# Down projections that read and write their 384 token columns in runs of 32

## The reference

```
def half_ffn(x, shift, scale, gate, g, w_gu, w_down):
    h = modulate(x, g, shift, scale)              # RMS norm, then scale and shift
    a, u = jnp.split(h @ w_gu, 2, axis=-1)        # w_gu: 1024 x 5632
    return x + FFN_RES * gate * ((jax.nn.silu(a) * u) @ w_down)    # w_down: 2816 x 1024

for i in range(DEPTH):
    xp = half_ffn(xp, ..., ff1_w_gu[i], ff1_w_down[i]);  xs = half_ffn(xs, ...)
    xp, xs = token mixer i (windowed, global, latent-compressed or neighbourhood attention)
    xp = half_ffn(xp, ..., ff2_w_gu[i], ff2_w_down[i]);  xs = half_ffn(xs, ...)
```

## Time and profile before

| what | value |
|---|---|
| median of 3 runs | 2933.23 us |
| span of the profiled execution, first to last instruction | 2931.5 us |
| median less that span | 1.7 us |
| PE busy | 2900.1 us, 99% of the span, 17613 matmuls |
| DVE busy | 2274.4 us, 78% |
| ACT busy | 1252.3 us, 43% |
| DMA, mean of the core's 16 engines | 167 GB/s |
| matmuls of the down projections | 3 x 1408 = 4224 |

### The profile page before, as it was taken

How to read it: one execution, slowest core, us unless ns; L and a number is a source line. 1 busy time by engine, 2 the same in 40 slices (tenths; PEclk the granted TensorE clock), 3 DMA queues, 4 the chain that set the end, 5 groups by cost and what they waited for, 6 DMA issues and landing times.

```text
span 2931.5 us, 44455 instructions
## 1 busy us (share of the span) xinstructions
PE 2900.1 (99%) x17613; PEld 2810.0 (96%) x17613; DVE 2274.4 (78%) x3459; ACT 1252.3 (43%) x2001; POOL 166.6 (6%) x171
## 2 busy tenths in 40 slices
PE   8999999999999999999999999999999999999999
PEld 6999979999999998999999997899999999989999
DVE  6889887888787877888788777778888887777653
ACT  3332464443333266443333348644333333664432
POOL 0000220000000030000000012000000001320000
PEclk9999999999999999999999999999999999999999
DMA  7555314555455512455455531255555555324342
GB/s 290 208 211 216 145 42 170 187 201 204 181 190 190 217 56 93 186 193 210 180 191 199 198 120 46 73 201 193 199 190 192 193 207 195 108 75 173 128 143 93
DMA packets 87722, 490.22 MB, mean 167 GB/s; under 512 B 11824, under 2 KB 13168, under 8 KB 51376
## 3 DMA queue, kind: packets, MB, share of 16 engines
q1 hardware_dynamic: 83696, 480.42, 44.4%
q0 software_dynamic: 3904, 8.24, 1.1%
HBM read 485.33 MB, written 3.29 MB: 167 GB/s over the span
## 4 chain that ended last, share of the span: by engine, by line
PE 55%; issue 38%; DVE 4%; ACT 1%; DMA 1%; POOL 1%; SPq 0%; DVEq 0%; POOLq 0%; ACTq 0%
PE ps L840 16%; PE ps L859 8%; PE ps L845 8%; PE ps L880 5%; PE ps L1060 4%; PE ps L863 4%; PE ps L824 1%; PE ps L995 1%; PE ps L1035 1%; DMA boot<-in_mod_w 1%; PE ps L1134 1%; PE ps L976 1%; PE ps L980 1%; DVE tmp L1685 0%; PE ps L1079 0%
## 5 line engine op out<-in xcount | busy, mean ns | idle before, releaser
L840 PE MATMUL ps<-h_hi,w_hi 128*128 128x386 f32 x2688 | 908.2, 338 | 0.0
L840 PE MATMUL ps<-h_lo,w_hi 128*128 128x386 f32 x2688 | 893.4, 332 | 0.0
L1593 DVE TENSOR_TENSOR w_lo<-w_raw,w_hi 128x2048 fp32r<-128x2048 f32 (+3 forms) x282 | 706.9, 2507 | 30.0 <-ACT w_hi L1263 29.6
L1613 DVE CUSTOM_DVE_ANT_0 F_junk<-F_slab,cond,mod_b 128x1024 f32<-128x1024 f32 x544 | 707.2, 1300 | 12.7
L1263 ACT ACTIVATE w_hi<-w_raw 128x2048 fp32r<-128x2048 f32 (+4 forms) x278 | 578.7, 2082 | 14.8 <-DMA w_raw<-in_ffn_dn 10.8
L840 PEld LDWEIGHTS ps<-h_lo,w_hi 128*128 128x128 f32 x2688 | 512.5, 191 | 0.0
L840 PEld LDWEIGHTS ps<-h_hi,w_hi 128*128 128x128 f32 x2688 | 503.1, 187 | 0.4 <-ACT w_hi L1263 0.4
L845 PE MATMUL ps<-h_hi,w_lo 128*128 128x386 f32 x2688 | 494.4, 335 | 0.0
L859 PE MATMUL ps<-F_act_hi,w_hi 128*128 128x384 f32 x1408 | 473.6, 336 | 0.0
L859 PE MATMUL ps<-F_act_lo,w_hi 128*128 128x384 f32 x1408 | 473.3, 336 | 0.0
L845 PEld LDWEIGHTS ps<-h_hi,w_lo 128*128 128x128 f32 x2688 | 469.0, 187 | 0.0
(11 more groups left out here) (371 smaller groups left out, 3465.9 us busy)
## 6 DMA issues: line engine op xcount, KB each, us to landing
w_raw<-in_ffn_gu SPq DMA_DIRECT2D x176, 1024.0 KB, 4.8
F_slab<-in_mod_w SPq DMA_DIRECT2D x272, 512.0 KB, 5.6
w_raw<-in_ffn_dn SPq DMA_DIRECT2D x64, 1408.0 KB, 6.4
w_raw<-in_d_w SPq DMA_DIRECT2D x8, 1536.0 KB, 6.7
boot<-in_mod_w SPq DMA_DIRECT2D x8, 1024.0 KB, 10.2
w_raw<-in_a_w SPq DMA_DIRECT2D x4, 1536.0 KB, 6.6
w_raw<-in_b_w SPq DMA_DIRECT2D x4, 1536.0 KB, 6.7
w_raw<-in_c_w SPq DMA_DIRECT2D x8, 544.0 KB, 3.6
```

The costliest lines, as they stand in the source:

```text
L840: pe.matmul(ps[:, 2 * par + u, 0:N_MOVE], w[0][:, k, u, :], h[:, k, :], start=(k == 0 and h is h_hi), stop=False)
L1593: dve.tensor_tensor(w_lo[par][:, 0:w], w_raw[par][:, 0:w], w_hi[par][:, 0:w], ALU.subtract).then_inc(w_split_lo.sem, 1)
L1613: dve.tensor_tensor_reduce(out=junk[:], in0=w, in1=cond[:, c, :], scale=scale, scalar=mod_b[:, n:n + 1], op0=ALU.mult, op1=ALU.add, accum_ ...
```

## The change

The function `combed` is new. It takes a tile of 384 consecutive columns and gives a view of the same columns in another order: four groups, and in each group a run of 32 columns of token tile 0, then one of tile 1, then one of tile 2. In the second feed-forward of a layer (`s % 3 == 2`) the groups rise: columns 0-31, 128-159, 256-287, then 32-63, 160-191, 288-319, and so on. In the first one (`s % 3 == 0`) they fall: 96-127, 224-255, 352-383, then 64-95, and so on. Within a run the columns always rise. The view is used for both the moving operand and the PSUM output, so each column still lands where it did. Weights, waits, semaphores, buffers and DMAs are as before.

```
+RUN = 32
...
+def combed(z, s):
+    n = P // RUN
+    step, at = (-RUN, (n - 1) * RUN) if s % 3 == 0 else (RUN, 0)
+    return bass.AP(tensor=z.tensor, offset=z.offset + at, ap=[list(z.ap[0]), [step, n], [P, TT], [1, RUN]])
...
                     for y in (act_hi, act_lo):
-                        pe.matmul(ps[:, B_DN[par], 0:N_TOK], w_hi[par][:, k * P:(k + 1) * P],
-                                  y[:, k * N_TOK:(k + 1) * N_TOK], start=(k == 0 and y is act_hi), stop=False)
+                        pe.matmul(combed(ps[:, B_DN[par], 0:N_TOK], s), w_hi[par][:, k * P:(k + 1) * P],
+                                  combed(y[:, k * N_TOK:(k + 1) * N_TOK], s), start=(k == 0 and y is act_hi), stop=False)
                 pe.wait_ge(w_split_lo.sem, w_split_lo.after(s, c))
                 for k in range(KF):
-                    mm = pe.matmul(ps[:, B_DN[par], 0:N_TOK], w_lo[par][:, k * P:(k + 1) * P],
-                                   act_hi[:, k * N_TOK:(k + 1) * N_TOK], start=False, stop=(k == KF - 1))
+                    mm = pe.matmul(combed(ps[:, B_DN[par], 0:N_TOK], s), w_lo[par][:, k * P:(k + 1) * P],
+                                   combed(act_hi[:, k * N_TOK:(k + 1) * N_TOK], s), start=False, stop=(k == KF - 1))
```

## The result

| | before | after |
|---|---|---|
| median | 2933.35 us (9 runs, 2932.97 to 2933.96) | 2941.15 us (9 runs, 2940.93 to 2941.92) |
| ratio | | 1.0026, 95% interval 1.0017 to 1.0036 |
| span of the profiled execution | 2931.5 us | 2939.4 us |

The change made the kernel slower by 7.8 us. The forecast was no effect, with 0.50; slower had 0.27. The time lies in the stated range, and the direction is wrong. The range was 57 us wide, for effects of another size or sign, so that it holds the result is no merit of the forecast.

What follows compares the result with a forecast made beforehand. PE, at full clock with no waits in the down projection, was taken to bound the kernel. Terms summed to 0 on a 2931.5 us span; with the median 1.7 us above it, 2933.2 us was forecast, range 2905 to 2962.

Steps and rivals of the forecast that it cites:

- no effect: Down projections keep their pace, the time staying within 0.2%, 5.9 us; the case forecast, chance 0.50.
- What bounds the kernel: PE, busy 99% at full clock without waits in layer 1's second down projection; matmul starts 173.3 ns apart set the time.
- (a): Columns streamed per down matmul: still 384, one a cycle, 160.0 ns; change 0.
- (b): Eleven turns within each down matmul, read and write side: taken as 0, upper end 8 ns a turn, 378 us.
- (d): Slow 44 matmuls of each stage's first down step may become ordinary, or settling take longer: 1.8 us at most, taken as 0.
- the prediction's own sign: If durations of L859, the down matmuls on w_hi, grow with the starts, the turns within a matmul are the failed step.
- (c): The 13.3 ns lost between down matmuls: taken as unchanged, 0; bounds −56 us and +22 to +26 us.
- (e): Other engines: ACT and DVE refill weight buffers, 12.0 us in two steps of 22.9 us, and stay hidden; change 0.
- The wider spacing: Rival: every down step after its first 44 matmuls slows by 5.1 to 6.1 ns a matmul, 2955 to 2959 us; chance 0.21.
- the sign of being wrong: Distance between down matmul starts moving by more than 1.4 ns on average.
- The faster case: Rival: part of the 13.3 ns between down matmuls goes; half gone 2905 us, all 2877 us; chance 0.23.
- the dear turns: Rival: each run in a down matmul served as its own stream, 8 ns a turn, +378 us, 3311 us; chance 0.06.

Runs made afterwards that it cites:

- e3: Kernel of before with rising runs of 32 in all stages and both activation tiles at eight different places: stages take 91.94, 93.27, 93.26 or 93.63 us.
- e4: Kernel of before, its column order kept, both activation tiles at eight different places, one per stage: stages take 92.63, 92.50, 91.57 or 91.35 us.
- e9: Changed kernel with runs of 64 columns instead of 32: 2933.28 us, ratio to before 0.9999, all eight stages 91.57 us.
- e1: Kernel of before with another order per stage: read side only 93.26 rising, 91.94 falling; output side only 91.57 us both ways; other forms 91.57 to 93.26.
- e5: Kernel of before with split down weights 48 columns further on, orders and activation places varied by stage: stages take 91.35 to 93.63 us.
- e6: Kernel of before, down matmuls loading 128, 64 or 32 weight columns, orders varied by stage: rising runs of 32 take 91.93 us at 64, 91.35 at 32.
- e12: Before's order with activations at place 56, down matmuls cut to 384 through 256 columns by stage: from 173.3 ns at 384 to 117.9 at 256.

## Why the prediction was wrong, point by point

**What bounds the kernel** held in seven of eight stages: PE has no wait in the down projections, before or after, and what a matmul takes longer reaches the end. In the first stage DVE ends later than PE, and some 0.5 us is hidden there. The earlier trace rows are of another stage and could not show that.

**Step (a)**, the columns streamed, held.

**Step (b)** is the step that failed, its term for the reads within a matmul: "What I take is 0". Without its slow first step a stage of before would take 91.57 − 0.22 = 91.35 us; against that the eight stages measured 4 x 0.59 + 4 x 1.91 = +10.0 us for (b), and 8 x 0.22 = 1.8 us less for term (d), together the 8.2. In the steps after the first, the runs show +1.7 ns for the `w_hi` matmuls and nothing for the `w_lo` ones in the falling stages, and +3.4 and +4.2 ns in the rising ones. The error is in one sentence: "Whatever repeats every 32 columns sees the same sequence as before." As far as it goes it is true, and it doesn't bear on the case, since what matters repeats every 64 columns (e3, e4), and the same argument with 64 is right (e9: nothing lost). I had inferred from the trace only that starts are regular, which does not give a period. The row I leaned on, L776, turns back by 128 columns, two whole periods, at half the column rate; it could not show this cost. By the prediction's own sign the step is (b) too: the durations grew with the starts, from 336 ns for L859 to 339 and 338:

```profile
L869 PE MATMUL ps<-F_act_lo,w_hi 128*128 128x384 f32 x1408 | 476.7, 339 | 0.0
L869 PE MATMUL ps<-F_act_hi,w_hi 128*128 128x384 f32 x1408 | 476.0, 338 | 0.0
```

Its upper end of 8 ns a turn was far off as well: 11 turns cost 4.2 ns together at most in the changed kernel.

Of the two rules of the Trainium skill that were weighed there, the first, on non-contiguous PSUM patterns, is not borne out for runs of 32: the output side alone made no difference (e1). I called the second page milder, which was a misreading: the Trainium skill's page Advanced Engine Details and Errata, section PSUM Cachelines, states the first rule as well, beside the one on every two elements. Runs shorter than 32 were tried on both sides at once only, so for them no run separates the output side.

**Step (c)** was right on the 13.3 ns: the loss remained in all 32-column orders. Its upper bound, +5.1 to +6.1 ns, had the right cause, a meeting of the moving read with the weight read, and contains the outcome, but what was taken is 0 here as well. The argument against it, that 173.3 ns comes back for tiles at different places, was wrong: at place 8 the order of before itself takes 175.4 and 176.5 ns (e4). Why the gate-and-up steps reach 173.3 ns at their places was not looked into.

**Step (d)** held in its bound of 1.8 us and not in the 0 that it took: the slow first step vanished in all stages, which gave back some 0.2 us each. It is in the stage times above.

**Step (e)** held; DVE and ACT are as busy as before.

**The rivals.** The wider spacing was right in its place, every down step, and in its cause, with 0.21. It put the price at 5.1 to 6.1 ns for every matmul; it was 3.4 to 4.2 in half of the stages and 1.7 or nothing in the others, because falling order stands 32 columns further on. So 2941 us came out and not 2955 to 2959. On average it is 8.2 us / 4224 = 1.9 ns a matmul, over the 1.4 ns that the prediction had named as the sign of being wrong; its sign for this rival, steps of 11.8 us or more, did not appear either (11.51 and 11.68). The faster case and the dear turns did not occur.

The forecast went to the case with no evidence against it rather than to the one whose mechanism was in the trace. Two spacings of 178.4 and 179.4 ns stood there, for instructions that otherwise start 173.3 ns apart, with no wait to explain them; an order that moves the reads of TensorE against each other in a stream with no slack had little room to be free, and the best of all tried places and orders gains only 0.2 us a stage over before.

The Trainium skill, page TensorE: Matmul & The Clock Gate, section Step-by-step: what each phase is for, says that weights and moving columns have two independent read ports and that loading the next weights takes no read bandwidth from the running matmul. For the fp32r streams of this kernel the runs disagree with the second point: moving the weights by 48 columns changes a stage by up to 1.7 us (e5), and with half of the weight columns the excess of rising runs falls from 1.69 to 0.26 us (e6).

## What to carry to other kernels

In a stream of fp32r matmuls with no slack, choose the free-dimension offset of the moving tile relative to the weight tile by measurement, modulo 64 columns (256 bytes). If the order must change, try runs of 64 first, which were free here. The wrong remainder cost 1.3 us in 91.6 for contiguous columns here. A pace that changes for a while in one trace, with no wait to explain it, means that the pace hangs on how reads fall together: take such a place as the likeliest to move when addresses are reordered. Where a program repeats a stage, give each repetition its own variant and read them all from one profile.

## What the runs showed of the hardware that was not expected

- The cost of an order of the moving columns repeats every 64 fp32r columns of place: 8 and 72, 24 and 88, 40 and 104, 56 and 120 gave the same stage times to 0.01 us, in two orders.
- For runs of 32 and for contiguous columns the steady cost follows the distance to the weights and not the place of the activations alone (e5), and for runs of 32 it goes with a shorter weight read (e6). What holds up the one read where it meets the other is not shown.
- Rising runs of 4 columns on both sides cost 20.7 ns a matmul (10.91 us / 527), and no less with a shorter weight read (e6); rising runs of 8 cost 8.7 ns (4.61 us / 527).
- A stepped output to PSUM in runs of 32 cost nothing that the profile shows (e1: 91.57 us in both directions).
- 382 columns took longer than 384: 174.1 against 173.3 ns (e12).
